# A two-layer decoder trunk: the shared expert by token inside the norm, sums opened ahead of the lists, last sums ahead of a branch, index scores moved back

## The reference, cut to what matters

```python
D_MODEL, SEQ, DEPTH, N_META = 1024, 256, 2, 16      # 272 tokens in the kernel
h = concat(meta, x)
for l in range(2):
    # mixer: sparse attention (8 heads, latent 128) and retention (4 heads), one output projection
    proj = h @ w_in[l]                 # qa, ckv, qi, ki, wi, qr, kr, vr, gr
    score[t,s] = sum_h wi[t,h] * relu(q_idx[t,h] . k_idx[s])    # indexer
    # each query attends to its 64 best causal keys
    h = layer_norm(alpha*h + mix @ w_o, ln1)
    # mixture of experts: sigmoid scores, 64 experts in 8 groups, 8 experts a token
    scores = sigmoid(h @ w_router);  grp/top-k choice;  gates = scores/sum * 2.5
    shared = (silu(h @ ws_gate) * (h @ ws_up)) @ ws_down        # hidden width 256
    h = layer_norm(alpha*h + routed + shared, ln2)
return h[:, 16:]
```

## Time and profile before

| what | value |
|---|---|
| median of 3 runs | 1557.39 us (1557.18 to 1558.21) |
| the profiled execution | 1557.55 us, its span 1555.7 us, mean granted clock 0.963 |
| TensorE matmul | 1479.8 us busy, 95% |
| TensorE weight load | 774.1 us, 50% |
| VectorE | 354.3 us, 23% |
| ScalarE | 252.6 us, 16% |
| GpSimd | 137.0 us, 9% |
| DMA, SyncE's queue | 442.32 MB, 71.5% of 16 engines' span |

### The profile page before, as it was taken

How to read it: one execution, slowest core, us unless ns; L and a number is a source line. 1 busy time by engine, 2 the same in 40 slices (tenths; PEclk the granted TensorE clock), 3 DMA queues, 4 the chain that set the end, 5 groups by cost and what they waited for, 6 DMA issues and landing times.

```text
span 1555.7 us, 21297 instructions
## 1 busy us (share of the span) xinstructions
PE 1479.8 (95%) x8413; PEld 774.1 (50%) x8413; DVE 354.3 (23%) x1109; ACT 252.6 (16%) x600; POOL 137.0 (9%) x163
## 2 busy tenths in 40 slices
PE   8899987999999999999978999789999999999996
PEld 5655553544544445445447645545454545444452
DVE  0621471111111111111144312611111111111112
ACT  1253110111111111111122430101111111111110
POOL 2031012000000000000000120110000000000000
PEclk9998899999999999999999978889999999999999
DMA  9521334999999999999934123249999999999990
GB/s 340 231 109 55 136 112 155 404 407 399 401 405 389 407 402 399 403 405 394 348 120 175 66 97 135 110 144 416 414 411 410 409 418 411 410 413 416 415 396 31
DMA packets 99826, 471.22 MB, mean 303 GB/s; under 512 B 11681, under 2 KB 13921, under 8 KB 66369
## 3 DMA queue, kind: packets, MB, share of 16 engines
q1 hardware_dynamic: 87760, 442.32, 71.5%
q0 software_dynamic: 12016, 28.27, 5.0%
HBM read 484.48 MB, written 3.35 MB: 314 GB/s over the span
## 4 chain that ended last, share of the span: by engine, by line
PE 45%; DVE 3%; issue 1%; ACT 1%; DVEq 0%; POOL 0%; ACTq 0%
PE bank L592 14%; PE bank L630 8%; PE bank L548 8%; PE bank L674 3%; PE bank L561 2%; PE bank L685 2%; PE bank L876 2%; PE bank L851 1%; PE bank L615 1%; PE bank L792 1%; PE bank L958 1%; PE bank L933 0%; PE bank L909 0%; PE bank L773 0%; PE bank L948 0%
## 5 line engine op out<-in xcount | busy, mean ns | idle before, releaser
L592 PE MATMUL bank<-ring,region 128*64 128x256 f32 x4096 | 453.0, 379 | 1.7 <-issue 1.7
L592 PEld LDWEIGHTS bank<-ring,region 128*64 128x64 f32 x4096 | 295.9, 137 | 174.2 <-issue 37.4
L548 PE MATMUL bank<-region 128*128 128x512 f32 x512 | 269.0, 610 | 6.3 <-issue 6.3
L630 PE MATMUL bank<-ring,region 128*64 128x512 f32 x1024 | 250.8, 611 | 2.4 <-ACT region L1060 1.4
L1414 DVE TENSOR_TENSOR region<-region,bank 128x256 f32<-128x256 f32 x64 | 27.0, 421 | 559.2 <-ACT region L1053 559.2
L1060 ACT ACTIVATE region<-bank 128x512 f32<-128x512 f32 x128 | 76.4, 597 | 475.9 <-PE bank L630 475.9
L1688 POOL DMA_INDIRECT region<-h_rows,rank_i x64 | 63.6, 994 | 938.4 <-DVE region L1392 879.0
L630 PEld LDWEIGHTS bank<-ring,region 128*64 128x64 f32 x1024 | 62.7, 137 | 163.8 <-issue 87.2
L548 PEld LDWEIGHTS bank<-region 128*128 128x128 f32 x512 | 78.5, 192 | 63.8 <-issue 63.8
L561 PEld LDWEIGHTS bank<-const,region 128*128 128x128 f32 x512 | 66.9, 195 | 67.6 <-ACT region L1044 42.7
L561 PE MATMUL bank<-const,region 128*128 128x128 f32 x512 | 90.3, 299 | 2.7 <-ACT region L1044 2.7
(11 more groups left out here) (193 smaller groups left out, 920.5 us busy)
## 6 DMA issues: line engine op xcount, KB each, us to landing
ring<-in_w_gate_dram SPq DMA_DIRECT2D x64, 2048.0 KB, 10.4
ring<-in_w_up_dram SPq DMA_DIRECT2D x64, 2048.0 KB, 12.7
ring<-in_w_down_dram SPq DMA_DIRECT2D x64, 2048.0 KB, 9.0
ring<-in_w_in_dram SPq DMA_DIRECT2D x8, 2048.0 KB, 17.4
ring<-in_w_o_dram SPq DMA_DIRECT2D x4, 2048.0 KB, 10.3
ring<-in_w_in_dram SPq DMA_DIRECT2D x4, 1024.0 KB, 8.5
ln_par<-in_ln_g_dram POOLq DMA_DIRECT2D x4, 512.0 KB, 5.5
ln_par<-in_ln_b_dram POOLq DMA_DIRECT2D x4, 512.0 KB, 7.1
```

What stands on the lines that cost most here:

```text
L548: last = mm(bank[SUM_BANKS[n][half]][0:w, :], selg[:, u, t0:t0 + w], y_sb[:, u, half * 512:(half + 1) * 512], start=False, stop=stop, skip ...
L592: last = mm(bank[5][64 * e:64 * e + 64, part * F:(part + 1) * F], xgT[:, u, kk, 64 * e:64 * e + 64], w[:, e, kk, :], start=(kk == 0), stop ...
L630: last = mm(bank[6][64 * e:64 * e + 64, :], mo["h2"][:, j * 128 + 64 * e:j * 128 + 64 * e + 64], w[:, e, j, half * 512:(half + 1) * 512], ...
```

## The change

- **Shared expert by token, among the norm's chunks.** The gate and up weights go side by side into one tile `wsgu` (512 columns for each of the 8 slices of the model width; their DMAs write pieces of 1 KB). The hidden values of a chunk of 128 tokens are 8 matmuls of 512 columns with `hT` as the weights; those of the meta tokens are 32 small ones. They are multiplied by VectorE and turned by TensorE (`turn_hidden`), two transposes a chunk, into `hsT`. The router runs in two parts: chunks 0 and 1 before chunk 2's rows are turned, then chunk 2, and its copy, turning and sigmoid likewise (`SCORED` counts them). Shared matmuls stand between these steps: one behind the first turning of scores, one behind the second router part, the rest of chunk 1 and half of chunk 2 ahead of the turned choice, the rest behind it.
- **Sums open ahead of the lists.** The sums of chunks 1 and 2 are opened, and chunk 1's shared output added, before `turn_lists`; chunk 2's and the meta tokens' behind it. VectorE multiplies chunk 1's hidden values ahead of the lists, chunk 2's behind the fifth of eight rounds, the meta tokens' when the lists are read.
- **Last sums ahead of the branch.** `last_sums` stands behind every round, ahead of the branch, and waits for its own sums; the counters are arranged for it (`extra_done`, `SCATTERS`).
- **Index scores of chunk 1 moved back**, behind `qa3`; the projection `qk1` stands whole behind the latent queries, and `FILL` starts at job 2 with `qk2`.
- `xhat` of the two norms, the lists, the indices and `hsT` have places of their own.

```diff
-FILL = [{1: ("qk1", 0, 4), 3: ("qk1", 4, 8), 5: ("qk2", 0, 4), 7: ("qk2", 4, 8), 8: ("qk0", 0, 8), 10: ("g1", 0, 4),
-         12: ("g1", 4, 8), 14: ("g2", 0, 4), 16: ("g2", 4, 8)} for l in range(DEPTH)]
-FILL[0][18] = ("g0", 0, 8)
+FILL = [{2: ("qk2", 0, 4), 4: ("qk2", 4, 8), 6: ("qk0", 0, 8), 8: ("g1", 0, 4), 10: ("g1", 4, 8), 12: ("g2", 0, 4),
+         14: ("g2", 4, 8)} for l in range(DEPTH)]
+FILL[0][16] = ("g0", 0, 8)
...
-SCORED = [2, 3]
+EXTRA_SUMS = [EXTRA * 5, EXTRA * 9]
+SCORED = [3, 5]
+SHARED = tally([[1, 2] + ([0] if l == 0 else []) for l in range(DEPTH)])
...
-                sp.dma_start(wsg, wsg_v[l:l + 1].rearrange("l p n -> (l p) n")).then_inc(ws_gate_up_in, 16)
-                sp.dma_start(wsu, wsu_v[l:l + 1].rearrange("l p n -> (l p) n")).then_inc(ws_gate_up_in, 16)
+                sp.dma_start(wsgu[:, :, 0:F], wsg_v[l:l + 1].rearrange("l p (k n) -> (l p) k n", k=KC)).then_inc(ws_gate_up_in, 16)
+                sp.dma_start(wsgu[:, :, F:2 * F], wsu_v[l:l + 1].rearrange("l p (k n) -> (l p) k n", k=KC)).then_inc(ws_gate_up_in, 16)
...
                 project_features("qa1", QA, 128, 128, lo)
-                index_scores(1, 8)
                 project_features("qa2", QA, 256, 128, lo)
                 project_features("qa3", QA, 384, 128, lo)
+                index_scores(1, 8)
...
+                pe.wait_ge(w_in_in[QK], l * 16 + 16)
+                project_tokens("qk1")
...
+                turn_h((l, 0), 1)
+                if l == 0:
+                    features_ready((l, 0), 0)
+                features_ready((l, 0), 1)
+                router(lo, 144)
+                turn_h((l, 0), 2)
+                turn_scores(QUERIES[l][:-1], 0)
+                pe.wait_ge(ws_gate_up_in, l * 32 + 32)
+                shared(1, 0, 1)
+                features_ready((l, 0), 2)
+                router(144, T)
+                shared(1, 1, 2)
+                turn_scores([2], 1)
+                shared(1, 2, KC)
+                shared(2, 0, 4)
...
+                last.then_inc(chosen_turned, 1)
+                shared(2, 4, KC)
+                if l == 0:
+                    shared(0)
...
                 pe.wait_ge(h_ready_tok, NORM[(l, 0)][2])
+                pe.wait_ge(ws_down_in, l * 16 + 16)
+                open_sums(1)
+                turn_hidden(1)
+                open_sums(2)
+                turn_hidden(2)
+                shared_down(1)
+                pe.wait_ge(score_ready, SCORED[l])
+                turn_lists(l * ROUNDS)
                 if l == 0:
+                    turn_hidden(0)
                     open_sums(0)
...
+                last = shared_down(2)
                 if l == 0:
-                    shared_down(0, 0)
...
+                    last = shared_down(0)
                 last.then_inc(scattered, 1)
                 hold_here(pe, count_ready, l + 1)
                 most = pe.value_load(count_i[0:1, 0:1], min_val=0, max_val=T)
-                round_(l, 0, False)
+                round_(l, 0)
+                last_sums(l, 0, sums_done, SUMMED[l][SUM_ORDER[l][-1]])
                 with pe.If(most > CAP):
...
+            def last_sums(l, r, done, value):
+
+                pe.wait_ge(y_ready, (l * ROUNDS + r) * 64 + 64)
+                pe.wait_ge(selg_ready, (l * ROUNDS + r) * 32 + 32)
+                for n, half in SUM_ORDER[l]:
+                    scatter(l, 1, n, half, stop=True).then_inc(done, 1)
+                hold_here(pe, done, value)
+                pe.sem_inc(scattered, 1)
...
+                shared_hidden(1)
                 dve.wait_ge(chosen_turned, l + 1)
...
-                make_lists(l, l * ROUNDS)
+                make_lists(l, l * ROUNDS, 0, 5)
+                shared_hidden(2)
+                make_lists(l, l * ROUNDS, 5)
```

More of the change, by code:

```diff
@@ L911, in _, with router, turn_scores @@
-                pe.wait_ge(router_copied, l + 1)
+                def router(t0, t1):
+                    for kk in range(KC):
+                        last = mm(bank[4][0:E, t0:t1], wr3[:, kk, :], hT[:, kk, t0:t1], start=(kk == 0), stop=(kk == KC - 1))
+                    last.then_inc(router_sums, 1)
+                def turn_scores(ns, part):
+                    pe.wait_ge(router_copied, l * 2 + part + 1)
+                    for n in ns:
+                        t0, w = CHUNKS[n]
+                        last = pe.transpose(bank[7][0:w, n * E:(n + 1) * E], mo["logitT"][0:E, t0:t0 + w], ident[0:E, 0:E])
+                    last.then_inc(router_done, 1)
@@ L1036, in layer_norm @@
                         normalise(l, ph, n)
+                if between:
+                    between()
                 if order[-1]:
@@ new lines, in _, with shared_gate @@
+                scores([2], 1)
+                def shared_gate(n):
+                    act.wait_ge(h_ready_tok, NORM[(l, 0)][1])
+                    act.wait_ge(shared_done, SHARED[l][n])
+                    w = CHUNKS[n][1]
+                    if n:
+                        act.activation(hidden[n], bank[7 - n][:, 0:F], ACT.Sigmoid).then_inc(shared_sig, 1)
+                    else:
+                        for q in range(2):
+                            last = act.activation(hidden[0][0:w, q * 128:(q + 1) * 128], bank[7][32 * q:32 * q + w, 256:384], ACT.Sigmoid)
+                        last.then_inc(shared_sig, 1)
```

227 lines of the change are left out of this document (116 added, 111 removed).

## The result

The changed kernel takes 1535.09 us in the median of 4 runs (1531.81 to 1536.28), the kernel before 1557.38 us (1557.18 to 1558.21): ratio 0.9853, 95% interval 0.9835 to 0.9870. Forecast were 1527.0 us, range 1518 to 1541: the sign and the range held. The time lies 8.1 us above the forecast and outside the narrower stretch (1520 to 1531) that the prediction gave one chance in two. The profiled execution took 1533.96 us, 23.6 less than that of before.

The account below looks back on a forecast made before the run. TensorE paces the expert loop, which the change leaves alone; gains lie in the stretches outside it. Terms 11.0 + 8.0 + 5.7 + 1.4 + 4.3 = 30.4 us off 1557.55, and 0.16 off, give 1527.0 us, range 1518 to 1541.

Parts of the forecast that it names:

- layer 1, norm to first pair: Layer 1 ahead of the expert loop: first transposes 12.9 us earlier, less 1.9 for the clock, net 11.0 us.
- layer 0, same stretch: Layer 0, norm to first pair: first transposes at 243.6 in place of 251.64, 8.0 us gained (7.0 to 8.8).
- attention, layer 0: Layer 0's attention: logits 3.6 us earlier by the reordered projections, 1.6 us (0 to 4) given back at the tail.
- attention, layer 1: Layer 1's attention: same steps as layer 0, 3.9 us gained, 0.2 us given back at the tail.
- last sums at the end: End of layer 1: last sums start at once, ahead of the branch, 1.4 us gained, wholly on the path.
- sums and change of layers: After layer 0: sums ahead of the branch bring layer 1's first projection from 796.77 to 792.4, 4.3 us (2.5 to 5.3).
- start of the index scores, loops: Expert loops: nothing inside them is touched, so they keep their length; no gain was counted.
- Rival B: Branch: the time belongs to the change from last y to sums, so moving sums gives nothing; 1532.5 us, chance 0.08.
- The front: Layer 0's attention up to the logits: qk1 done at 86.5 in place of 90.1, 3.6 us gained.
- Rival A: Clock falls at both routers, layer 0's last shared sums, layer 1's first pair, layer 0's retention; 1534 us, chance 0.20.
- Rival C: Attention gives back: VectorE's later choice bounds, clock stays low, -3 us a layer; 1539 us, chance 0.11.
- rival D: Stretch ahead of the pairs: gather and lists set it, only the lists' 0.7 and 2.9 us remain; 1542, chance 0.06.

Follow-up runs that it names:

- late gate projection: Changed kernel with chunk 0's gate projection in layer 0 put back from attention job 16 to job 18: 1528.97 us, ratio 0.9816 to the kernel before.
- hold in the arms: Changed kernel with the wait for its last sums, and the count behind it, moved from ahead of the branch into its two arms: 1529.61 us, ratio 0.9825.

## Why the prediction was right, and where it was 7 us off

By its own terms, forecast and found in the profiled executions:

| term | forecast | found |
|---|---|---|
| layer 1, norm to first pair | 11.0 (12.9 less 1.9) | 10.6 (12.3 less 1.7) |
| layer 0, same stretch | 8.0 | 6.7 |
| attention, layer 0 | 2.0 | 0.5 |
| attention, layer 1 | 3.7 | 3.5 |
| last sums at the end | 1.4 | 1.3 |
| sums and change of layers | 4.3 | 0.7 |
| start of the index scores, loops | 0 | 0.6, -0.4 |
| sum | 30.4 | 23.5 |

- **The mis-sized term** is the change of layers, 3.6 of the 6.9 us. The mechanism was named: the added wait for the sums keeps TensorE's sequencer from running ahead. Its price was read from the chain's 3.59 us, the part of the jump that stuck out. The jump was 6.17 us long and 2.6 of it lay beside the last down matmuls and the copy of y behind them. The hold puts it wholly behind the sums. The row that would have shown it was in the trace of before: the jump's own row on TensorE's sequencer, with its start. Moving the hold alone returned 3.86 us.
- **Rival B** is not what happened, though after layer 0 the gain is as small as it said: the time is bound to the jump, and at the end of layer 1, where nothing stands behind the jump, the 1.3 us came. The page of the Trainium skill that was weighed there, Advanced Engine Details and Errata, section Control Flow Timing, gives about 0.1 us for a compare and branch. ScalarE's and VectorE's took 50 and 63 ns here, about half of it; TensorE's 3.3 to 6.2 us are far above it, and the measurement decides.
- **Layer 0's attention** was off by more than its sum shows, and that is luck. The front was forecast at 3.6 us and brought 6.1, since the 2 us of half clock charged to qk1 did not come in this kernel. What goes back at the tail was forecast at 1.6 us (0 to 4) and came to 5.6: 2.1 in the last jobs and 3.5 from retention on. The two errors of 2.5 and 4.0 us nearly cancel. The direction of the second was right: the clock falls ahead of retention. The late gate projection showed that it is the place of that one projection among the jobs, not the moved index scores, that opens the waits: with it back in its old place the 6.0 us stayed.
- **Layer 0 ahead of the pairs**: the forecast's 1.5 us between full and half clock at the last shared sums. They took 6.31 us, at full clock 4.69 (the kernel with the late gate projection). The 7.0 to 8.8 forecast missed by 0.3.
- **Layer 1** came out step by step, both the 12.9 us and the loss at the first pair. The wait that takes the place of the old ones is the gather's, 1.14 us for 1.7.
- **Rival A**, the clock, had its time nearest (1534) and two of its four places: retention of layer 0 (3.5 us up to the norm) and that layer's last shared sums (1.6). The routers ran at full clock and the first pair lost only what the forecast had. **Rival C** is out (attention gained 4.0 together), **rival D** is out by the 12.3 us.

## What to carry to other kernels

Before a hold or a wait is put in front of a branch, read the branch's own row on that engine's sequencer, and count its whole length, not the part that shows now. Where TensorE waits ahead of dense work and the rows behind the wait run at 1.2 GHz, the wait costs itself and those rows; real work that can stand there, or failing that columns nobody reads, gave back 2.5 to 3.6 us a place at four places here. At two others the columns gave nothing: where the rows behind ran at full clock anyway, and where they no longer fitted into the wait. Read such edits by stage: medians of single edits differed from their stage's gain by up to 3 us and did not add up.

## What the runs showed that was not expected

- TensorE's jump over the further rounds took 3.28 to 4.95 us at the end of layer 1, 5.2 to 6.2 after layer 0 with the loads of weights beside it and 3.4 to 3.5 with them held back; the same compare and branch on the other engines took 0.05 to 0.06.
- Retention lost the full clock some microseconds after its start in every kernel profiled, though no row of it shows a wait of over 0.51 us. Without the longer waits ahead of it, the fall came some 4 to 6 us behind the start of its first transposes and not ahead of them. Why it falls there stays open.
- Two kernels that differ in one wait can differ by a microsecond or more at a stage that the edit doesn't touch (layer 0 in the kernel with the hold in the arms: 194.7 us against 191.8). Part of it sits at the latent queries and qk1: the first logits of layer 0 came 31.4, 32.4 to 32.8 or 34.4 us after the first index scores, in kernels with the same edits up to there.
